# RWKV short sequences of a hybrid decoder trunk: eight heads at a time against all sixteen at once

## The reference

```
def rwkv7_recurrence(r, decay, k, v, a, b, s0):
    def step(S, inp):
        r_t, w_t, k_t, v_t, a_t, b_t = inp
        sa = jnp.einsum('bhij,bhj->bhi', S, a_t)
        S = S * w_t[:, :, None, :] + sa[..., None] * b_t[:, :, None, :] + v_t[..., None] * k_t[:, :, None, :]
        return S, jnp.einsum('bhij,bhj->bhi', S, r_t)
    S, y = lax.scan(step, s0, xs)
```

## Time and profile before

| what | value |
|---|---|
| median of three runs | 3194.11 us |
| the profiled execution | 3197.23 us |
| its span, first to last instruction | 3195.4 us |
| PE busy, share of the span | 2789.5 us, 87% |
| prompt scan | 2284 to 2496.8 us |
| short sequences | 2496.8 to 2650.4 us |
| group norm and gate | 2650.4 to 2697.4 us |

### The profile page before, as it was taken

One profiled execution on the slowest core, in us unless ns is written; L12 is line 12 of the kernel. 1 busy time (PEld: TensorE's weight loads), 2 busy tenths in 40 slices (PEclk: granted clock), 3 DMA queues, 4 the chain that ended last, 5 costly groups with the idle time before them and its releaser, 6 DMA issues.

```text
span 3195.4 us, 60747 instructions
## 1 busy us (share of the span) xinstructions
PE 2789.5 (87%) x26393; PEld 2618.5 (82%) x26393; DVE 1242.2 (39%) x1468; ACT 866.6 (27%) x1185; POOL 1078.7 (34%) x514
## 2 busy tenths in 40 slices
PE   7999989787887899998999986875588677899997
PEld 6999989767865899998999976873488544899997
DVE  2333158715534433313333223335745325433312
ACT  3222232222212322223222222234133102422221
POOL 3444323314412244432444422322734011344432
PEclk9999989998978999999999998877699768999998
DMA  3223212210021222221222211210000001122221
GB/s 130 86 85 97 81 63 79 68 42 2 2 86 59 67 85 85 100 91 53 86 85 93 91 61 54 66 34 30 2 4 4 25 27 33 61 90 86 95 91 46
DMA packets 59724, 201.86 MB, mean 63 GB/s; under 512 B 14512, under 2 KB 14640, under 8 KB 59312
## 3 DMA queue, kind: packets, MB, share of 16 engines
q1 hardware_dynamic: 59568, 199.51, 18.8%
HBM read 189.81 MB, written 9.67 MB: 62 GB/s over the span
## 4 chain that ended last, share of the span: by engine, by line
PE 42%; issue 33%; POOL 11%; DVE 11%; ACT 1%; DMA 1%; DVEq 0%; POOLq 0%; SPq 0%; ACTq 0%
POOL wlo L258 10%; PE ps L288 9%; PE ps L286 9%; PE ps L287 9%; DVE cb L802 3%; PE ps L2032 1%; PE ps L2416 1%; PE ps L2040 1%; PE ps L553 1%; PE ps L2442 1%; DVE sFM L2211 1%; PE ps L1983 1%; PE ps L2443 1%; PE ps L1988 1%; PE ps L558 1%
## 5 line engine op out<-in xcount | busy, mean ns | idle before, releaser
L258 POOL TENSOR_TENSOR wlo<-raw,whi 128x1024 fp32r<-128x1024 f32 (+1 forms) x316 | 835.3, 2645 | 1516.2 <-ACT whi L250 1516.2
L286 PE MATMUL ps<-xh,whi 128*128 128x272 f32 x3776 | 1106.4, 293 | 61.5 <-POOL wlo L258 40.6
L288 PE MATMUL ps<-xh,wlo 128*128 128x272 f32 x3776 | 1104.6, 293 | 0.0
L287 PE MATMUL ps<-xl,whi 128*128 128x272 f32 x3776 | 1097.8, 291 | 0.0
L286 PEld LDWEIGHTS ps<-xh,whi 128*128 128x128 f32 x3776 | 722.2, 191 | 77.2 <-POOL wlo L258 38.9
L287 PEld LDWEIGHTS ps<-xl,whi 128*128 128x128 f32 x3776 | 724.1, 192 | 0.0
L288 PEld LDWEIGHTS ps<-xh,wlo 128*128 128x128 f32 x3776 | 721.7, 191 | 0.0
L250 ACT ACTIVATE whi<-raw 128x1024 fp32r<-128x1024 f32 (+1 forms) x316 | 354.4, 1124 | 1275.1 <-PE ps L288 1228.3
L288 PE MATMUL ps<-mh,wlo 128*128 128x272 f32 x1408 | 406.1, 288 | 0.0
L287 PE MATMUL ps<-ml,whi 128*128 128x272 f32 x1408 | 405.4, 288 | 0.0
L286 PE MATMUL ps<-mh,whi 128*128 128x272 f32 x1408 | 405.0, 288 | 0.0
(11 more groups left out here) (440 smaller groups left out, 3094.5 us busy)
## 6 DMA issues: line engine op xcount, KB each, us to landing
raw<-w SPq DMA_DIRECT2D x252, 512.0 KB, 3.5
raw<-w SPq DMA_DIRECT2D x64, 704.0 KB, 4.0
h<-xT SPq DMA_DIRECT2D x1, 2176.0 KB, 11.4
yT<-h SPq DMA_DIRECT2D x1, 2176.0 KB, 6.6
Sst<-state_gdn SPq DMA_DIRECT2D x4, 512.0 KB, 3.6
SG<-state_gdn SPq DMA_DIRECT2D x4, 512.0 KB, 3.6
gdn_s_s<-gG SPq DMA_DIRECT2D x4, 512.0 KB, 2.7
gdn_s_s<-gT SPq DMA_DIRECT2D x4, 512.0 KB, 2.6
```

Of the source, the lines that this page charges most:

```text
L258: pool.tensor_tensor(wlo[two][:, 0:kt * P], raw[slot][:, 0:kt * P], whi[two][:, 0:kt * P].bitcast(F32), ALU.subtract).then_inc(w_lo, 1)
L286: pe.matmul(o, wh, hi[:, r, :], start=(start and k == 0), stop=False)
L287: pe.matmul(o, wh, lo[:, r, :], start=False, stop=False)
L288: mm = pe.matmul(o, wl, hi[:, r, :], start=False, stop=(stop and k == kt - 1))
```

## The change

The group loop is gone; all 16 heads go through one pass (`short_*`). The states are fetched before the scan, into the space of the four `raw` buffers, all eight tiles in one buffer `S0`, and the decay and the change are applied in place. ACT packs a and r (`qAR`), b and k (`qBKs`) and v (`qVS`) as 64 columns, 32 of each. One 64x64 product per head gives all token pairs (`qGR`, masked once). The state is read by 64x64 products, one per head and sequence, that add up in PSUM over the sequences: `qAM` holds a and r spread so that each sequence's columns are zero but its own. The inverse is replaced by four substitutions: four times `qUV` = product of `qGR` and `qUV`, plus the read-out `qWQs`. The change of the states is one 64x512 product per head. The first four units of `wo` are no longer loaded before the scan; all eight are loaded when the states have been written. `rpost` is unchanged except for its waits.

```diff
+        AR, BKs, VS, BKe, GR, BKt, UV, WQs = (place("q" + n, [P, NM, 64], F32, at) for n in
+        AM = place("qAM", [P, NM, NB, 64], F32, at)
+        at = [raw_at]
+        S0 = place("S0", [P, NM, NB, 64], F32, at)
+        short = place("short", [P, SHORT.shape[1]], F32, at)
...
         def scan_dve(dve):
             scan_ready(dve)
             dve.wait_ge(W["cm"], past(W["cm"], 1))
-            dve.memset(RS[:, :, :], 0.0)
             dve.memset(St[0][:, :, :], 0.0).then_inc(W["s_up"], 1)
...
+        def short_pe(pe):
+            short_ready(pe)
...
+            pe.wait_ge(R["q_ar"], past(R["q_ar"], 4))
+            for m, pr in heads(range(NM)):
+                mm = pe.matmul(ps[pr, 0, 64 * m:64 * m + 64], BKs[pr, m, :], AR[pr, m, :], start=True, stop=True)
+            mm.then_inc(R["q_g_mm"], 1)
...
+                mm = pe.matmul(ps[pr, 2, 64 * m:64 * m + 64], VS[pr, m, :], M["ident"][pr, pr], start=True, stop=True)
+            mm.then_inc(R["q_v_mm"], 1)
+            consts_in(pe)
+            for m in range(NM):
+                pe.wait_ge(R["q_am"], past(R["q_am"], m + 1))
+                for b in range(NB):
+                    for par in range(2):
+                        pr = own(par)
+                        mm = pe.matmul(ps[pr, 3 + 4 * (m // 4), 64 * (m % 4):64 * (m % 4) + 64], AM[pr, m, b, :], S0[pr, m, b, :],
+                                       start=(b == 0), stop=(b == NB - 1))
+                mm.then_inc(R["q_wq_mm"], 1)
...
+            for it in range(TS):
+                for hf in range(2):
+                    if it:
+                        pe.wait_ge(R["q_n"], past(R["q_n"], 2 * it + hf - 1))
+                    for m, pr in heads(range(4 * hf, 4 * hf + 4)):
+                        mm = pe.matmul(ps[pr, 4 + hf, 64 * (m % 4):64 * (m % 4) + 64], GR[pr, m, :], UV[pr, m, :], start=True, stop=True)
+                    mm.then_inc(R["q_n_mm"], 1)
...
+                    mm = pe.matmul(ps[pr, 6 + m % 2, :], BKt[pr, m, :], AM[pr, m, :, :].rearrange("p b t -> p (b t)"), start=True, stop=True)
+                mm.then_inc(R["q_ds_mm"], 1)
...
+        def short_act(act):
+            short_ready(act)
+            for dst, lo, src in ((AR, 0, RA), (AR, NS, r_), (BKs, 0, RB), (BKs, NS, k_), (VS, NS, v_)):
+                act.activation(dst[:, :, lo:lo + NS], whole(src)[:, :, TP:T], ACT.Copy).then_inc(R["q_ar"], 1)
...
+        def short_dve(dve):
...
+            def spread(m):
+                dve.tensor_tensor(AM[:, m, :, :], AR[:, m, :].unsqueeze(1).broadcast_to([P, NB, 64]), tokmask, ALU.mult).then_inc(R["q_am"], 1)
+            spread(0)
+            spread(1)
+            dve.wait_ge(R["q_g_mm"], past(R["q_g_mm"], 1))
+            dve.tensor_tensor(GR[:, :, :], bank64(0), gmask2.unsqueeze(1).broadcast_to([P, NM, 64]), ALU.mult).then_inc(R["q_g"], 1)
+            for m in range(2, NM):
+                spread(m)
+            for it in range(TS):
+                for hf in range(2):
+                    dve.wait_ge(R["q_n_mm"], past(R["q_n_mm"], 2 * it + hf + 1))
...
+                        up = dve.tensor_tensor(UV[rows, ms, :], bank64(4 + hf)[rows, 0:4, :], WQs[rows, ms, :], ALU.add)
+                    up.then_inc(R["q_n"], 1)
...
+            def masked(m):
+                dve.tensor_tensor(AM[:, m, :, :], UV[:, m, :].unsqueeze(1).broadcast_to([P, NB, 64]), over(rowmask, 64),
+                                  ALU.mult).then_inc(R["q_uvm"], 1)
+            def add(m):
+                dve.wait_ge(R["q_ds_mm"], past(R["q_ds_mm"], m + 1))
+                dve.wait_ge(R["q_se"], past(R["q_se"], m + 1))
+                dve.tensor_tensor(S0[:, m, :, :], S0[:, m, :, :], ps[:, 6 + m % 2, :].rearrange("p (b t) -> p b t", b=NB), ALU.add).then_inc(R["q_add"], 1)
+            masked(0)
+            for m in range(NM):
+                if m + 1 < NM:
+                    masked(m + 1)
+                add(m)
+        def short_pool(pool):
...
+                pool.tensor_tensor(dst, src, e, ALU.mult).then_inc(R["q_be"], 1)
+            consts_in(pool)
+            for m in range(NM):
+                pool.wait_ge(R["q_wq_mm"], past(R["q_wq_mm"], m + 1))
+                pool.tensor_tensor(S0[:, m, :, :], S0[:, m, :, :], over(ECE[:, m, 8:16], 64), ALU.mult).then_inc(R["q_se"], 1)
+        def short_load_sp(sp):
+            sp.wait_ge(w_lo, BASE["wo"])
+            for m in range(NM):
+                sp.dma_start(S0[:, m, :, :], a["state_rwkv"][m]).then_inc(R["q_in"], 16)
...
+        def short_sp(sp):
...
+            for m in range(NM):
+                sp.wait_ge(R["q_add"], past(R["q_add"], m + 1))
+                sp.dma_start(a["rwkv_s_s"][m], S0[:, m, :, :]).then_inc(R["q_out"], 16)
+            sp.wait_ge(R["q_out"], past(R["q_out"], 16 * NM))
+            load_units(sp, "wo")
...
         def rpost_pe(pe):
-            pe.wait_ge(R["ys_up"], past(R["ys_up"], NM))
-            pe.wait_ge(R["ss_add"], past(R["ss_add"], NM))
+            pe.wait_ge(R["ys_up"], past(R["ys_up"], 1))
```

More of the change, by code:

```diff
@@ L107, in masks, with short_masks @@
     return f, list(m), g, list(lo), seq
+def short_masks():
+    row, tok, both = np.arange(P) % 64, np.arange(NS), np.arange(2 * NS)
+    s = row % NS
+    same = s[:, None] // TS == tok[None, :] // TS
+    return np.concatenate([same & (s[:, None] < tok[None, :]), same & (s[:, None] <= tok[None, :]),
+                           np.repeat((np.arange(NB)[:, None] == both[None, :] % NS // TS).reshape(1, -1), P, 0),
+                           s[:, None] // TS == np.arange(NB)[None, :],
+                           (row[:, None] >= NS) & (s[:, None] == tok[None, :])], 1).astype(np.float32)
+SHORT = short_masks()
 RESET = np.ones((P, T), np.float32)
@@ L2325, in rstep_pe @@
[L2325 to L2331, removed]
-                    for par in range(2):
[L2333 to L2355, removed]
-            pe.wait_ge(R["l2_up"], past(R["l2_up"], n + 1))
-            levels = 2
-            inv_pe(pe, RI, Q, n, levels, nt)
-            for a_ in range(2):
-                pe.wait_ge(RI["fup"], RI["base"]["fup"] + inv_at(RI, n, levels, a_)[0] + 1)
-            pe.wait_ge(R["l4_up"], past(R["l4_up"], n + 1))
-            for s, tl, pr in heads():
-                mm = pe.matmul(ps[0:nt, 6, tl * P:(tl + 1) * P][:, pr], Q["L2"][0:nt, s, 0:nt], Vt[0:nt, tl, pr], start=True, stop=True)
-            mm.then_inc(R["gv_mm"], 1)
-            for s, tl, pr in heads():
-                mm = pe.matmul(ps[pr, 7, tl * P:tl * P + nt], Att[0:nt, tl, pr], Q["F"][0:nt, s, 0:nt], start=True, stop=True)
-            mm.then_inc(R["wt_mm"], 1)
-            pe.wait_ge(R["gv_cp"], past(R["gv_cp"], n + 1))
-            for s, tl, pr in heads():
-                mm = pe.matmul(ps[0:nt, 0, tl * P:(tl + 1) * P][:, pr], Q["F"][0:nt, s, 0:nt], GV[0:nt, tl, pr], start=True, stop=True)
-            mm.then_inc(R["u_mm"], 1)
-            pe.wait_ge(R["wt_cp"], past(R["wt_cp"], n + 1))
@@ L2375, in rst, with consts_in, own, first @@
-        def rst(i):
-            return (RS if i % 2 == 0 else SB1)
-        def rst_in(eng, i):
-            eng.wait_ge((R["si0"], R["si1"])[i % 2], past((R["si0"], R["si1"])[i % 2], 32 * (i // 2 + 1)))
-        def rsample_sp(sp):
+        def consts_in(e):
+            e.wait_ge(R["q_in"], past(R["q_in"], 16 * (NM + 1)))
+        def own(par):
+            return slice(64 * par, 64 * par + 64)
+        def first(par):
+            return slice(64 * par, 64 * par + NS)
+        gmask2 = short[:, 0:64]
@@ new lines, in short_dve @@
+        def short_dve(dve):
+            short_ready(dve)
+            dve.memset(VS[:, :, 0:NS], 0.0).then_inc(R["q_zero"], 1)
+            consts_in(dve)
+            dve.wait_ge(R["q_ar"], past(R["q_ar"], 2))
+            def spread(m):
[7 more added lines that the diff above has]
+            for it in range(TS):
+                for hf in range(2):
+                    dve.wait_ge(R["q_n_mm"], past(R["q_n_mm"], 2 * it + hf + 1))
+                    if it == 0:
+                        dve.wait_ge(R["q_wq_cp"], past(R["q_wq_cp"], hf + 1))
+                    for par in range(2):
+                        rows, ms = first(par), slice(4 * hf, 4 * hf + 4)
+                        up = dve.tensor_tensor(UV[rows, ms, :], bank64(4 + hf)[rows, 0:4, :], WQs[rows, ms, :], ALU.add)
+                    up.then_inc(R["q_n"], 1)
+            dve.wait_ge(R["q_n"], past(R["q_n"], 2 * TS))
+            def masked(m):
[10 more added lines that the diff above has]
+                add(m)
@@ L2584, in rwkv_pe @@
             scan_pe(pe)
-            for g in range(2):
-                rstep_pe(pe, g)
-                rsample_pe(pe, g)
+            short_pe(pe)
             rpost_pe(pe)
```

274 lines of the change are left out of this document (65 added, 209 removed).

## The result

The changed kernel took 3076.41 us (median of 4 runs, 3073.8 to 3077.95), the kernel before 3194.57 beside it: ratio 0.9628, 95% interval 0.9611 to 0.9645. Forecast were 3075.5. The profiled execution took 3077.95 us, its span is 3076.2.

The account below looks back on a forecast made before the run. The stage was taken as one chain, eight tiles long, over four engines with a DMA. A new 35.3 us chain saves 118.3, the memset 0.3: 3194.1 - 118.6 = 3075.5 us, range 3067 to 3094.

Parts of the forecast that it names:

- first block: PE's product for all token pairs, starting after four ACT copies of 256 columns: 1.6 us (1.2 to 2.4).
- V turn: PE's turn of v, sixteen 64x64 products after the token pairs: 0.96 us, ending at 3.5.
- rounds: Four substitution rounds of two halves, paced by DVE: first product 0.65, then 6.7 us, ending at 20.6.
- outputs: 32 products of 32 columns on PE between substitution and first change: 1.9 us (1.0 possible), ending at 22.5.
- the extras: Added to the chain: eight further hand-overs 0.9, POOL's copy of `halves` 0.5, one PE stop in mid-run 1.4 us.
- The clock at nothing: PE's blocks in the stage priced at the fast 0.96 us, not the lower clock's 1.77.
- The low-clock rival (+15): Rival: PE's clock stays low throughout the new stage, about +15 us, 3091; chance 0.13.
- DVE and POOL at +1.0: In the read-out, DVE's last four spreads alternate with four POOL decays, so PE's last block starts 1.0 us later.
- POOL's +9.2: Rival: DVE and POOL hold each other up longer, six spreads at 2.66 us each; +9, 3085; chance 0.08.
- The halves in turn: Rival: two heads writing one PSUM bank run in turn on PE, not together; 3090; chance 0.04.
- The costs put at nothing: Fetches and masks ahead of the scan, later `wo` loads, early `g2w`: no time charged.
- The memset removed from the scan: Dropping DVE's `RS` memset (0.91 us) ahead of a mask PE waits for saves 0.3 us (0 to 0.9).

Follow-up runs that it names:

- the one with one half: Changed kernel with the read-out's products reordered, per tile eight batches of the even head, then eight of the odd; 3083.97 us, ratio 0.9656.
- the three-part one: Changed kernel with the outputs' products between the changes, two filler products on PE, and packs of B and k on DVE; 3076.42 us, ratio 0.9616.
- the run with late fetches: Changed kernel with the eight state tiles and masks fetched inside the stage, after the scan, instead of during it; 3086.30 us, ratio 0.9658.

## Why the prediction was right

The sum was right to 0.5 us (35.3 forecast, 34.8 measured), and its steps mostly so. The chain was the right one, with its steps in the right order; that the sum came so close is luck, since the errors of its terms cancel. From the scan's last add, forecast and measured: first block at 1.6 and 1.6; end of the V turn 3.5 and 4.2; end of the read-out 12.2 and 12.5; end of the turn of b and k 13.2 and 13.4; end of the rounds 20.6 and 21.1; of the outputs 22.5 and 23.1; first add 23.5 and 25.1; DVE's end 32.5, with the extras 35.3, and 34.8.

Three terms were mis-sized and cancel:

- *The clock at nothing.* The V turn took 1.63 for 0.96, the read-out 8.3 for 7.7, the first change some 0.9 more, the adds behind it 0.45 more than at the high clock (9.74 for 9.29 from the first add to the end): +2.7 us. The low-clock rival (+15) did not come as a whole; parts of it did, in most executions of one pass, though not in the one with one half nor in the three-part one. My reason, that the scan pauses as often and has 0.95, did not carry over to this stage.
- *DVE and POOL at +1.0.* Nothing of it reached the path. Of eight spreads only one was long (minimum 680, median 683, maximum 1530 ns): the slow V turn and the slow start of the read-out had put off POOL's first decay to 2504.31, when only the last spread was still to begin. At the high clock the term is real: four of six spreads were long, PE waited, and holding POOL back returned 1.2 us. So the step was right in kind, and hidden here by the clock.
- *Extras at 2.8.* The copy of `halves` (2521.84, 1.04 long) fell into DVE's wait for the first change, and PE had no stop in mid-run here: -1.9 us. The hand-overs came nearly as priced (0.9): the rounds took 0.35 more than their term, the adds 0.3 more at the high clock. Part of the latter is a step that the sum lacked: the last change has only one DVE operation beside it, and DVE waits 0.58 for it.

Two rivals' sums are off by 1.0 us each, which the forecast does not feel. POOL's +9.2 counts from a last block at 10.2, where the sum already had 11.2, so it is +8.2. The halves in turn would have hidden POOL's 1.0, as the low clock does. And of the rows behind the 0.64 of a spread, L2189 has an input in PSUM; the spreads alone took 0.68, starting 0.6 apart.

The costs put at nothing held. PE waited for no fetch. SP's first `wo` load started at 2535.62, three us after the last add, and ACT split it at 2578.62. The rounds were paced by DVE as forecast: sixteen operations in 7.0 us, PE waiting 0.2 per half (the row on L2312). The 512-column products, two heads on half of the array each, took 0.86 a pair: in the run with late fetches PE's timeline has two pairs of heads in 1.93 with the tail:
```profile
2531.14 1.93 PE L2321 MATMUL ps<-qAM,qBKt 64*64 64x512 f32 x8
```
The Trainium skill, TensorEngine Tiling (Array Packing), section Restrictions and Gotchas, excludes two row tiles in one bank at one time; by it this would be 3.4, an estimate from four products of 0.86 in turn. The traces disagree for the two heads on their two halves: 0.96 for sixteen products of 64 columns, 1.93 for the four of 512.

The memset removed from the scan cannot be told from what else moved there: 2.2 us less for the whole scan, 0.3 forecast. No run of the changed kernel needed the range's upper end (3094); its slowest took 3077.95.

## What to carry to other kernels

Price a stage along its one longest chain, from the last instruction ahead of it to the first behind it, and check each landmark; a sum that is right may have terms that cancel. A step on all heads in one block gains by fewer hand-overs and by one wait for a transfer in place of several, and in these runs its longer pieces on PE went with a higher clock. Before you move a block off the path, ask what lay beside it: the block of 1.9 us gave 1.1.

## What the runs showed of the hardware

- A spread that met one of POOL's decays took about 0.85 us longer: 4.54, 5.38, 6.23 and 7.08 us for six in the different runs (3.69 alone). POOL's decays were then longer too, up to 1.49 us for 1.04. Beside POOL's shorter operations on `qBKe` the loss was smaller: the first two spreads took 2.09 us in the three-part run, 1.29 in the changed kernel.
- The same products had a granted clock of 0.90 to 1.00 in one pass, 0.78 and 0.83 in two, and 0.54 in eight. That the shorter pieces are the reason was not shown.
- Two products of 512 columns in PE's pause did not save the clock in the stage: 6.8 us of it were at the lower level with them and without. The three-part run has the same two products and was at 1.00 throughout.
